# Delta rule in a two-block model kernel: W and Q times the state as one product, output per pair of chunks, squares turned instead of multiplied

## What is computed

```python
def _gated_delta_chunked(q, k, v, g, beta):
    ...
    gc = jnp.cumsum(g, axis=-1)
    diff = gc[..., :, None] - gc[..., None, :]
    kb = k * beta[..., None]
    L = jnp.where(strict, jnp.einsum("bhncd,bhnsd->bhncs", kb, k)
                  * jnp.exp(jnp.where(strict, diff, 0.0)), 0.0)
    rhs = jnp.concatenate([v * beta[..., None], kb * jnp.exp(gc)[..., None]], axis=-1)
    sol = lax.linalg.triangular_solve(eye + L, rhs, left_side=True, lower=True,
                                      unit_diagonal=True)
    u, w = sol[..., :dv], sol[..., dv:]
    a_qk = jnp.where(incl, jnp.einsum("bhncd,bhnsd->bhncs", q, k)
                     * jnp.exp(jnp.where(incl, diff, 0.0)), 0.0)
    qg = q * jnp.exp(gc)[..., None]
    kd = k * jnp.exp(g_last[..., None] - gc)[..., None]
    ...
    def step(S, inp):
        qg_c, kd_c, u_c, w_c, a_c, d_c = inp
        v_new = u_c - jnp.einsum("bhck,bhkv->bhcv", w_c, S)
        o = (jnp.einsum("bhck,bhkv->bhcv", qg_c, S)
             + jnp.einsum("bhcs,bhsv->bhcv", a_c, v_new))
        S = S * d_c[..., None, None] + jnp.einsum("bhck,bhcv->bhkv", kd_c, v_new)
        return S, o
```

## Time and profile before

| | us |
|---|---|
| median of three runs | 880.71 |
| the profiled execution | 881.82 |
| its span, first to last instruction | 880.0 |
| PE busy in it | 859.8 |
| DVE busy | 623.1 |
| ACT busy | 509.1 |
| POOL busy | 73.6 |

### The profile page before, as it was taken

The page is one execution under the profiler, slowest core; times in us unless marked ns, Lnnn a source line. Parts: engine busy times, 40 slices in busy tenths (PEclk is TensorE's granted clock), DMA queues, the critical chain, the costliest instruction groups (busy, mean ns, idle before and its releaser), DMA issues.

```text
span 880.0 us, 14646 instructions
## 1 busy us (share of the span) xinstructions
PE 859.8 (98%) x5816; PEld 780.8 (89%) x5816; DVE 623.1 (71%) x1124; ACT 509.1 (58%) x826; POOL 73.6 (8%) x76
## 2 busy tenths in 40 slices
PE   6999999999999999999999999999999999999997
PEld 6999999999989999999998799999999776778885
DVE  6787987988867766666656787787456455775765
ACT  5565777665377656656657688544444434454443
POOL 0200002001020211111113000500000000000000
PEclk9999999999999999999999999999999999999999
DMA  9457443457455655555564555643322322365541
GB/s 344 146 194 276 159 145 108 169 179 291 140 186 174 239 190 175 187 191 175 185 198 137 181 188 201 222 145 124 117 97 96 113 104 96 119 205 195 197 146 48
DMA packets 40588, 149.21 MB, mean 170 GB/s; under 512 B 4524, under 2 KB 4680, under 8 KB 39880
## 3 DMA queue, kind: packets, MB, share of 16 engines
q1 hardware_dynamic: 40520, 148.27, 49.3%
HBM read 147.18 MB, written 1.08 MB: 168 GB/s over the span
## 4 chain that ended last, share of the span: by engine, by line
PE 89%; DVE 5%; ACT 3%; issue 1%; DMA 1%; SPq 0%; DVEq 0%; ACTq 0%
PE bank L610 40%; PE bank L605 16%; PE bank L606 16%; PE bank L607 16%; PE bank L613 2%; DVE t_wl L1739 2%; DVE t_arena L1744 1%; DVE t_arena L1754 1%; DVE t_x L1754 1%; ACT t_hh L1237 1%; DMA t_x<-in_xin 1%; DVE t_sm L1751 1%; ACT t_arena L1237 1%; ACT t_wh L1232 0%; ACT t_br L1237 0%
## 5 line engine op out<-in xcount | busy, mean ns | idle before, releaser
L1739 DVE TENSOR_TENSOR t_wl<-t_raw,t_wh 128x1024 fp32r<-128x1024 f32 x260 | 316.5, 1226 | 114.3 <-ACT t_wh L1232 113.4
L1232 ACT ACTIVATE t_wh<-t_raw 128x1024 fp32r<-128x1024 f32 x260 | 273.4, 1058 | 129.1 <-PE bank L610 60.3
L605 PE MATMUL bank<-t_hh,t_wh 128*128 128x256 f32 x1144 | 330.3, 289 | 2.2 <-DVE t_hl L1744 1.5
L607 PE MATMUL bank<-t_hh,t_wl 128*128 128x256 f32 x1144 | 323.6, 283 | 0.0
L606 PE MATMUL bank<-t_hl,t_wh 128*128 128x256 f32 x1144 | 323.5, 283 | 0.0
L605 PEld LDWEIGHTS bank<-t_hh,t_wh 128*128 128x128 f32 x1144 | 219.1, 192 | 6.1 <-issue 4.2
L606 PEld LDWEIGHTS bank<-t_hl,t_wh 128*128 128x128 f32 x1144 | 219.2, 192 | 0.8
L607 PEld LDWEIGHTS bank<-t_hh,t_wl 128*128 128x128 f32 x1144 | 219.1, 192 | 0.0
L610 PE MATMUL bank<-t_wh,t_br 128*128 128x512 f32 x384 | 123.8, 393 | 0.2 <-POOL t_br L2448 0.2
L1754 DVE SCALAR_TENSOR_TENSOR t_arena<-bank,t_par,t_arena 128x255 f32<-128x255 f32 (+2 forms) x184 | 75.3, 474 | 45.0 <-ACT t_arena L1237 44.7
L610 PE MATMUL bank<-t_wh,t_hh 128*128 128x512 f32 x224 | 92.0, 411 | 1.8 <-DVE t_wl L1739 1.8
(11 more groups left out here) (152 smaller groups left out, 840.3 us busy)
## 6 DMA issues: line engine op xcount, KB each, us to landing
t_raw<-in_ws SPq DMA_DIRECT2D x260, 512.0 KB, 3.9
t_br<-decay SPq DMA_DIRECT2D x1, 2048.0 KB, 8.3
t_arena<-in_post SPq DMA_DIRECT2D x3, 512.0 KB, 5.5
t_arena<-gates SPq DMA_DIRECT2D x1, 1536.0 KB, 10.5
t_x<-in_xin SPq DMA_DIRECT2D x4, 256.0 KB, 5.5
t_bd<-in_bd SPq DMA_DIRECT2D x1, 1024.0 KB, 11.7
t_x<-in_xtok SPq DMA_DIRECT2D x1, 1024.0 KB, 5.8
t_arena<-in_mem SPq DMA_DIRECT2D x1, 1024.0 KB, 8.0
```

The costliest lines, as they stand in the source:

```text
L605: e.matmul(o, wh, xh, start=first, stop=False, skip_group_check=True)
L607: return e.matmul(o, wl, xh, start=False, stop=last, skip_group_check=True)
L1232: e.activation(WH[q % NS][:, :], RAW[q % NR][:, :], ACT.Copy, bias=0.0, scale=1.0).then_inc(*hi.now(q))
L1739: e.tensor_tensor(WL[q % NS][:, :], RAW[q % NR][:, :], WH[q % NS][:, :].bitcast(F), SUB).then_inc(*lo.now(q))
```

## The change

- The squares' transposes (`sq00t`, `sq01t`, `sq10t`, `sq11t`) are made by transposing what ScalarE has copied out of the bank of the square, in place of a second product. TensorE waits for that copy (`a_dn`) first.
- The strict mask is put into the block masks once, by GpSimd in a new function `block_masks` (during chunk `pl0`): the constant `strict` becomes "strictly above, inside a 16-block", `b16` becomes "strictly below, inside a 16-block". The two operations that masked `DLT` are gone; `dtb` is made from `DLT` with the new mask one tick earlier, and `tl` is also one tick earlier, behind `lb`.
- For chunks 1 to 3, W and the scaled query stand side by side as one stationary operand `WQ[c]` of 128 columns: ScalarE copies W's 64 columns from the bank, GpSimd the query's 64. `vn{c}` gives W times S in one half of the bank's rows and Q times S in the other; VectorE takes the first from U, ScalarE copies the second into `OTK`.
- The chunk's own output is one product of full size per pair of chunks, `o0` and `o1`; VectorE adds it to `OTK`. The rows of chunk 0 in `OTK` are set to zero by GpSimd.
- `DN_SEQ` follows. The update of S waits for `kv{c}`, not for `o{c}`.

```diff
-for _c in range(4):
-    DN_SEQ += ([(f"vn{_c}", "D")] if _c else []) + ([(f"kv{_c}", "D")] if _c < 3 else []) + [(f"o{_c}", "A")]
+DN_SEQ += [("kv0", "D"), ("vn1", "A"), ("kv1", "D"), ("o0", "D"), ("vn2", "A"), ("kv2", "D"), ("vn3", "A"), ("o1", "D")]
...
+        WQ = {1: WK[1][:, 0, :, :], 2: WK[1][:, 1, :, :], 3: WK[3][:, 0, :, :]}
...
-                yield from walk.until(179)
+                yield from walk.until(178)
                 for hf in range(2):
-                    e.wait_ge(*d_dn.of("strict", hf))
+                    e.wait_ge(*d_dn.of("lb", 3, 1))
                     ps = PB[dn_bank(f"tl{hf}")]
...
                         if level < 2:
                             yield
-                            prods(f"sq{level}{hf}t", hf, d, dT)
+                            e.wait_ge(*a_dn.of(f"sq{level}{hf}n"))
+                            turn(f"sq{level}{hf}t", [d2[:, hf, h, :] for h in range(4)])
...
                         e.wait_ge(*d_dn.of("s", c))
+                        e.wait_ge(*g_dn.of("q", c))
                         ps = bank(f"vn{c}")
                         for h in range(4):
-                            m = mm(ps[r, 128 * h:128 * h + 128], W_[:, hf, h, r], S[:, h, :])
+                            m = mm(ps[:, 128 * h:128 * h + 128], WQ[c][:, h, :], S[:, h, :])
                         m.then_inc(*p_dn.now(f"vn{c}"))
...
+                    if c == 1:
                         yield
-                    ps = bank(f"o{c}")
-                    for h in range(4):
-                        o = ps[r, 128 * h:128 * h + 128]
-                        if c > 0:
-                            mm(o, QKV[:, h, 64 * c:64 * c + 64], S[:, h, :], h == 0, False)
-                        m = mm(o, ET[r, hf, h, r], U[r, hf, h, :], c == 0 and h == 0, True)
-                    m.then_inc(*p_dn.now(f"o{c}"))
+                    if c % 2:
+                        prods(f"o{hf}", hf, ET, U)
...
-                    empty(f"w{hf}", W_[:, hf, :, :])
-                for c in range(4):
-                    hf, r = c // 2, slice(64 * (c % 2), 64 * (c % 2) + 64)
-                    yield from walk.until(198 + 2 * c)
-                    e.wait_ge(*p_dn.of(f"o{c}"))
-                    act(OTK[r, hf, :, :], heads(dn_bank(f"o{c}"))[r, :, :], ACT.Copy).then_inc(*a_dn.now(f"o{c}"))
-                    if c % 2 == 1:
+                    e.wait_ge(*p_dn.of(f"w{hf}"))
+                    for c in (1,) if hf == 0 else (2, 3):
+                        r = slice(64 * (c % 2), 64 * (c % 2) + 64)
+                        m = act(WQ[c][:, :, r], heads(dn_bank(f"w{hf}"))[:, :, r], ACT.Copy)
+                    m.then_inc(*a_dn.now(f"w{hf}"))
+                for c in range(1, 4):
+                    hf, r, o = c // 2, slice(64 * (c % 2), 64 * (c % 2) + 64), slice(64 - 64 * (c % 2), 128 - 64 * (c % 2))
+                    yield from walk.until(197 + 2 * c)
+                    e.wait_ge(*d_dn.of(f"vn{c}"))
+                    act(OTK[r, hf, :, :], heads(dn_bank(f"vn{c}"))[o, :, :], ACT.Copy).then_inc(*a_dn.now(f"vn{c}"))
+                    if c > 1:
                         yield from walk.until(199 + 2 * c)
-                        e.wait_ge(*a_dn.of(f"o{c}"))
-                        head_squares(OTK[:, hf, :, :], KT, OSUM, hf, a_dn.now("osq", hf))
+                        e.wait_ge(*d_dn.of(f"o{c - 2}"))
+                        head_squares(OTK[:, c - 2, :, :], KT, OSUM, c - 2, a_dn.now("osq", c - 2))
...
                 yield from walk.until(178)
+                e.wait_ge(*g_const.of("strict"))
                 e.wait_ge(*d_dn.of("lb", 3, 1))
                 for hf in range(2):
-                    tt(DLT[:, hf, :, :], DLT[:, hf, :, :], MASKS["strict"], MUL).then_inc(*d_dn.now("strict", hf))
+                    tt(WK[1][:, hf, :, :], DLT[:, hf, :, :], MASKS["strict"], MUL).then_inc(*d_dn.now("dtb", hf))
                 yield from walk.until(179)
                 for hf in range(2):
                     e.wait_ge(*a_dn.of(f"tl{hf}"))
                     tt(WK[0][:, hf, :, :], DL[:, hf, :, :], MASKS["b16"], MUL).then_inc(*d_dn.now("db", hf))
-                for hf in range(2):
-                    e.wait_ge(*d_dn.of("strict", hf))
-                    tt(WK[1][:, hf, :, :], DLT[:, hf, :, :], MASKS["b16"], MUL).then_inc(*d_dn.now("dtb", hf))
...
                     elif c < 3:
-                        e.wait_ge(*p_dn.of(f"o{c}"))
+                        e.wait_ge(*p_dn.of(f"kv{c}"))
...
+                    if c > 1:
+                        e.wait_ge(*p_dn.of(f"o{c - 2}"))
+                        e.wait_ge(*a_dn.of(f"vn{2 * c - 3}"))
+                        if c == 2:
+                            e.wait_ge(*g_dn.of("zero"))
+                        tt(OTK[:, c - 2, :, :], OTK[:, c - 2, :, :], heads(v_of(f"o{c - 2}")), ADD).then_inc(*d_dn.now(f"o{c - 2}"))
...
+            def block_masks():
+
+                up, low = cn("strict"), cn("b16")
+                e.wait_ge(*d_const.of("incl"))
+                tt(up, low, up, MUL).then_inc(*g_const.now("strict"))
+                tt(low, low, ident, SUB).then_inc(*g_const.now("off"))
+                e.wait_ge(*g_const.of("off"))
+                tt(low, low, up, SUB).then_inc(*g_const.now("strict"))
...
+                for c in range(1, 4):
+                    yield from walk.until(194 + c)
+                    r = slice(64 - 64 * (c % 2), 128 - 64 * (c % 2))
+                    e.wait_ge(*p_dn.of("inv641"))
+                    e.tensor_copy(WQ[c][:, :, r], QKV[:, 0:4, 64 * c:64 * c + 64]).then_inc(*g_dn.now("q", c))
+                e.wait_ge(*p_dn.of("w1"))
+                e.memset(OTK[0:64, 0, :, :], 0.0).then_inc(*g_dn.now("zero"))
```

More of the change, by code:

```diff
@@ L925, in dn_lane @@
                         prods(f"inv{name}{hf}", hf, Mq, Y)
-                U, W_ = WK[0], WK[1]
+                U = WK[0]
                 for hf in range(2):
@@ L2526, in pool_program @@
             walk.tick()
-            for i in range(4):
+            walk.cols("pl0")
+            block_masks()
+            for i in range(1, 4):
                 walk.cols(f"pl{i}")
```

## The result

The changed kernel takes 871.32 us, median of 4 runs (869.32 to 871.67), beside 880.62 us (880.42 to 880.88) for the kernel before: a ratio of 0.9886, with a 95% interval of 0.9873 to 0.9900. That is 9.3 us less. Forecast were 9.8 us less and 870.9 us. The profiled execution took 871.67 us with a span of 869.8 us.

What follows compares the result with a forecast made beforehand. TensorE's own work list plus its waits was taken as the bound. Savings of 10.65 us minus waits of 0.3 and 0.5 gave about 9.8 us, so 880.7 becomes 870.9 us, range 869.2 to 874.9.

Steps and rivals of the forecast that it cites:

- Squares: Four square products on TensorE become transposes, 0.35 us a group in place of 0.81: 1.84 us saved.
- Outputs: TensorE's output products: two full-size groups, 1.69 us, replace four groups of small products, 9.66 us: 7.97 us saved.
- W and Q: vn1 to vn3 with 128 stationary columns in place of 64: 0.14 us less each, 0.42 us saved.
- uncut units: Two weight units no longer cut in their middle by o0 and o2: 0.21 us each, 0.42 us saved.
- Step (a): Each turn waits for ScalarE to empty the square; only the first, near 610 us, uncovered: 0.3 us, bounds 0 and 1.5.
- Step (b): Three block_masks operations on GpSimd behind the LRU lane slow busy VectorE: 0.5 us on the path, bounds 0 and 2.
- (c): GpSimd's query copies before vn1 to vn3, and copies and memset beside VectorE's splits: zero, upper bound 1 us for the latter.
- (d): ScalarE's copies of vn1 to vn3 and VectorE's two additions, with weight splits behind them: zero added wait.
- The clock: Rival: transposes and waits near 610 us halve TensorE's clock over 608 to 632 us, up to 24 us more, 895 us; chance 0.02.

Runs made afterwards that it cites:

- run without alternation: Kernel before, with the eight output products of chunks 1 to 3 reordered, the state's four first, then the chunk's own four: 878.91 us, ratio 0.9972.
- version with earlier masks: Kernel with block_masks moved into the FFN, plus VectorE making the two cq32 masks between inv20 and inv21: 869.73 us, repeated 869.72 us.
- The turns alone: Kernel before with only the four square products replaced by transposes, its masks left as they were: 881.65 us, ratio 1.0002.
- masks in the FFN: Changed kernel with GpSimd's block_masks moved from chunk pl0 into the feed-forward part, after unit fu12: 870.57 us, ratio 0.9874.
- more masks: Changed kernel with six more GpSimd operations of the same kind and size right behind the three of block_masks: 871.50 us, ratio 0.9883.
- last changed kernel: Changed kernel unaltered, run once more beside the repeat of the version with earlier masks: 870.01 us, ratio 0.9870.

## Why the prediction was right, point by point

**Squares.** Forecast 1.84 us. The four turns are 0.46 us shorter each, and the kernel with products in their place is 1.82 us longer on TensorE. Right.

**Outputs, W and Q, uncut units.** Forecast 7.97 + 0.42 + 0.42 = 8.81 us; the timeline shows 11.38 - 1.84 = 9.54 us. The mechanism was right and the size 0.7 us short. From start to start, the output groups save 9.66 - 1.61 = 8.05 us (forecast 7.97), and the three wide `vn` groups 0.13 us each, with 0.07 us in the short pieces behind them (forecast 0.42). Both were sized well. The rest, about 1.0 us, lies in the weight units, and there I had 0.42: this is the term that was mis-sized. An uncut unit runs 2.86 us (701.41 to 704.27), so 0.31 us shorter than the cut one, not 0.21. And the units around the new `o0` and `o1`, which I had counted at nothing, got shorter too: the half in front of `o0` from 1.59 to 1.50 us (710.29 to 711.79), the half behind it from 1.59 to 1.46 us. For a small-tile group also costs its neighbour: the weight piece in front of it runs 0.32 us from start to start (708.89 to 709.21 us, changed kernel) where one in front of a full group runs 0.23 us (711.56 to 711.79). The unit of the earlier trace rows from which I took the 2.96 us stands between two such groups.

The Trainium skill, "TensorE: Matmul & The Clock Gate", Part 3 (packing small matmuls), says that products run at once if they have different parts of the array. I drew from it that the four 64 x 64 products would hide, and that was a stretch: the state's product takes all 128 rows, and the chunk's own four all sit at one position. The run without alternation agrees with this narrower reading: 2.04 us for eight, none hidden.

**Step (a), the first turn.** Forecast 0.3 us, bounds 0 and 1.5. It is 0. ScalarE starts the softmax at 608.03 us of the changed kernel, 0.61 us earlier than before on a clock that is 1.1 us late, and empties the square's bank in time:

```profile
604.71 1.28 DVE L1746 TENSOR_TENSOR t_arena<-t_bd,t_con 128x512 f32<-128x512 f32 x2
...
608.03 0.37 ACT L1478 ACTIVATE t_pw<-bank,t_sm 128x128 f32<-128x128 f32 x1 [4.49 <-DVE t_sm L1753]
...
610.45 0.60 ACT L1235 ACTIVATE t_arena<-bank 128x512 f32<-128x512 f32 x1
```

It is out at 611.05 us and the turn starts at 611.25: 0.2 us to spare. The 1.1 us by which this kernel is late do not explain that, for ScalarE is late by them too: in the version with earlier masks, which has no such loss at 160 us, the bank is out at 609.85 us and the turn starts at 610.05, again 0.2 us. What was mis-sized is the way of the masks. Counted from the place of `sq00t` (610.13 us before, 611.25 after), the softmax starts 1.73 us earlier, and I had 1.25 + 0.2. The two masks gave their 1.2 us. The transposes a tick earlier gave 0.5 us and not 0.2: VectorE starts its masks at 604.71 - 1.12 = 603.59 us where it started at 604.11, since it no longer stands 1.02 us in front of them waiting for ScalarE. The turns alone show the other end, 1.43 us.

**Step (b), the masks beside VectorE.** Forecast 0.5 us, bounds 0 and 2, and measured 0.7 us. The mechanism held and the place did not. I looked for it at 189 us, where TensorE already waited, but it fell due at 159 us, at the next weight split. The three operations took 2.06 us where I had put 1.1 from their size, and VectorE lost 0.70 us in that time: a third of it, where I had taken half. One by one they took 0.46, 0.77 and 0.79 us: the second and third came behind operations of VectorE.

The Trainium skill, "SBUF — State Buffer", section "Who interferes with whom", says that a VectorE instruction with two SBUF inputs contends with a GpSimd instruction that reads SBUF. Its section "Summary: rules for kernel authors" says that the second one to issue is blocked until the first has finished. The rows of single operations agree with both: the GpSimd operation that came behind a split ended 0.31 us after it (1.32 us instead of 0.46), and the split at 157.27 us, which came behind a GpSimd operation that ran to 157.60 us, took 0.22 us more than 1.20.

**Steps (c) and (d).** Zero, and zero, as forecast: between the first correction product and the last output TensorE has no new wait. The 0.8 us wait in front of `cq32` stayed, as forecast, and the run with earlier masks shows what it took to end it.

**The clock.** It was at 1.00 from 600 to 745 us; the rival falls.

**The sum.** 11.4 us off the list and 0.7 us of new wait are 10.7 us, where I had 9.8. The list was 0.7 us better and the two waits together 0.1 us shorter than forecast, but by two errors that cancel: (a) was 0.3 us too long and (b) 0.2 us too short. The measured differences, 9.3, 10.8 and 11.5 us in three comparisons, scatter by more than my error. Executions with the same mean granted clock lie closer: at 0.997 the medians are 881.45 us (23 of the kernel before, 880.60 to 882.06) and 871.21 us (5 of the changed kernel, 869.89 to 871.36), at 0.999 they are 880.05 (3) and 869.99 us (5), at 0.995 882.40 (10) and 871.67 us (1). So the change is worth 10.1 to 10.7 us. That the first comparison gave 9.3 us, next to 9.8, is therefore partly luck.

## What to carry to other kernels

Cost a piece of TensorE's list by the distance from its start to the next piece's start, and look at the weight loads inside it: a stop in front of each change of tile shape is a price that no single duration shows, and ordering products by shape wins part of it back without any other change (2.5 of the 8.6 us that the three groups took). Two changes that look independent can be one: the turned squares were worth 1.84 us here only with the masks part beside them, and about 0.2 us without. A small operation put on GpSimd was paid for by VectorE where VectorE was busy throughout, so it belongs where VectorE has slack, not where it is free on GpSimd. And before a merged row is divided by its count, its operations are to be looked at one by one: the six of 4.74 us were not six of 0.79, but took 0.46 to 1.32 us.

## What the runs showed of the hardware

Behind 560 us in the kernel before, a change between the 128x64 and 64x64 tiles stopped the weight load for 0.17 us each time, and so did one from either of them back to a full tile. From a full f32 tile to a small one it stood for 0.33 to 0.37 us in all places but one. Four f32 products of 128 x 128 took 0.80 to 0.89 us, and four with 64 columns 1.02 us, which includes one stop.

A GpSimd operation on 128x128 with nothing in its way took 0.46 us; one that started behind a VectorE split of 1.42 us took 1.32 us.

The first 20 us and the end of the FFN are not the same in two executions of one kernel. Rows of the stretch from 12 to 22 us (columns as above), first of the kernel with the masks in the FFN, then of the one with more masks:

```profile
12.00:22.00 10.00, 8.77 (x49) 8.59 (x48) 8.52 (x22) 5.27 (x8) 0.00 (x0) 0.66 1.02 414
```

```profile
12.00:22.00 10.00, 10.00 (x80) 10.00 (x80) 9.19 (x23) 6.39 (x10) 0.00 (x0) 1.00 1.02 409
```

Both kernels do the same there, but one is at the full clock and has 80 matmuls through where the other, with 0.66, has 49. At 24 us the thirteen traces lay up to 3.9 us apart, and the three of the changed kernel alone 1.2 us. Between 470 and 560 us three traces gained 0.5 to 0.6 us on the others: those of the masks in the FFN, of more masks and of the last changed kernel. They have a clock of 1.00 from 486 to 494 us, and the other ten 0.79. The whole time goes with this: the kernel before took 882.11 to 882.63 us in its ten executions with a mean clock of 0.995 and 879.82 to 880.48 us in its three with 0.999. With changes of a microsecond or less it was the shift between two traces after the first weight units that told the cases apart, or executions of the same mean clock, and not the median.
